# A two-layer encoder trunk on one core: sums of MLP weight blocks made by adding transfers in device memory, with 15 instead of 14 up-projection pairs per layer in seven products

## The reference, cut to what matters

```python
def sq_relu_mlp(y, w_up, w_down):
    u = y @ w_up                              # w_up (1024, 4096), w_down (4096, 1024)
    return jnp.square(jax.nn.relu(u)) @ w_down

for i in range(DEPTH):
    y = rmsnorm(h, norm_gains[i, 0])
    y = mlstm_mixer(y, ...) if i % 2 == 0 else diff_attention(y, ...)
    h = h + y
    h = h + sq_relu_mlp(rmsnorm(h, norm_gains[i, 1]), mlp_w_up[i], mlp_w_down[i])
```

## Time and profile before

| | |
|---|---|
| median of 3 runs | 1207.79 us (1207.68 to 1208.81) |
| the profiled execution's own span | 1205.8 us |
| PE busy | 1195.9 us (99%) |
| DVE busy | 895.2 us (74%) |
| ACT busy | 643.8 us (53%) |
| POOL busy | 62.1 us (5%) |
| DMA | 110.40 MB, 92 GB/s over the span |

### The profile page before, as it was taken

The page is one execution under the profiler, slowest core; times in us unless marked ns, Lnnn a source line. Parts: engine busy times, 40 slices in busy tenths (PEclk is TensorE's granted clock), DMA queues, the critical chain, the costliest instruction groups (busy, mean ns, idle before and its releaser), DMA issues.

```text
span 1205.8 us, 22165 instructions
## 1 busy us (share of the span) xinstructions
PE 1195.9 (99%) x8700; PEld 1133.4 (94%) x8700; DVE 895.2 (74%) x1446; ACT 643.8 (53%) x1117; POOL 62.1 (5%) x105
## 2 busy tenths in 40 slices
PE   9999999999999999999999999999999999999998
PEld 8999999999999999999999999987798998988988
DVE  6788788789479479488568888887984885875863
ACT  6777876744234244234357887777552352443453
POOL 3211120000000000001010000000000000000000
PEclk9999999999999999999999999999999999999999
DMA  7333333232323323323222122212333333242322
GB/s 179 91 100 95 88 91 93 86 95 86 126 71 105 106 71 105 105 73 117 75 81 77 54 70 65 83 44 76 99 105 105 104 107 105 71 141 70 96 79 71
DMA packets 143123, 110.40 MB, mean 92 GB/s; under 512 B 22152, under 2 KB 142016, under 8 KB 143040
## 3 DMA queue, kind: packets, MB, share of 16 engines
q1 hardware_dynamic: 141600, 104.93, 29.2%
q0 software_dynamic: 1312, 4.22, 1.3%
q10 hardware_dynamic: 128, 0.09, 0.0%
HBM read 107.11 MB, written 2.13 MB: 91 GB/s over the span
## 4 chain that ended last, share of the span: by engine, by line
PE 81%; ACT 8%; DVE 6%; issue 3%; DMA 1%; ACTq 0%; DVEq 0%; POOLq 0%
PE ps L2061 32%; PE ps L2115 23%; PE ps L1828 17%; PE ps L2332 2%; ACT dmat L756 1%; PE ps L2188 1%; DVE wl L1176 1%; DVE plo L1317 1%; ACT wh L660 1%; PE ps L2167 1%; PE ps L2166 1%; ACT qhs L660 1%; PE ps L2176 1%; ACT vh L660 1%; ACT phi L660 1%
## 5 line engine op out<-in xcount | busy, mean ns | idle before, releaser
L2061 PE MATMUL ps<-al,hi 128*128 128x264 f32 (+1 forms) x736 | 192.6, 318 | 0.0
L2061 PE MATMUL ps<-ah,hi 128*128 128x264 f32 (+1 forms) x736 | 192.6, 318 | 0.0
L2061 PE MATMUL ps<-ah,lo 128*128 128x264 f32 (+1 forms) x736 | 192.2, 318 | 0.0
L660 ACT ACTIVATE hi<-raw 128x1024 fp32r<-128x1024 f32 (+1 forms) x128 | 119.6, 957 | 133.9 <-PE ps L2061 133.9
L1828 PE MATMUL ps<-yh,wh 128*128 128x264 f32 (+1 forms) x704 | 160.4, 302 | 0.0
L1828 PE MATMUL ps<-yh,wl 128*128 128x264 f32 (+1 forms) x704 | 155.3, 295 | 0.0
L1828 PE MATMUL ps<-yl,wh 128*128 128x264 f32 (+1 forms) x704 | 155.2, 294 | 0.0
L2061 PEld LDWEIGHTS ps<-ah,hi 128*128 128x128 f32 x736 | 121.4, 188 | 10.0
L2061 PEld LDWEIGHTS ps<-al,hi 128*128 128x128 f32 x736 | 121.4, 188 | 9.8
L2061 PEld LDWEIGHTS ps<-ah,lo 128*128 128x128 f32 x736 | 121.2, 188 | 9.8
L2115 PE MATMUL ps<-th,hi 128*128 128x264 f32 (+1 forms) x448 | 126.6, 283 | 0.0
(11 more groups left out here) (295 smaller groups left out, 2729.2 us busy)
## 6 DMA issues: line engine op xcount, KB each, us to landing
raw<-in_mlp_w_up_dram SPq DMA_DIRECT2D x32, 1024.0 KB, 5.4
raw<-in_mlp_w_down_dram SPq DMA_DIRECT2D x32, 1024.0 KB, 5.2
raw<-in_diff_w_in_dram SPq DMA_DIRECT2D x24, 512.0 KB, 3.8
raw<-in_mlstm_w_in_dram SPq DMA_DIRECT2D x16, 512.0 KB, 5.0
raw<-in_mlstm_w_in_dram SPq DMA_DIRECT2D x16, 256.0 KB, 5.5
raw<-in_mlstm_w_out_dram SPq DMA_DIRECT2D x3, 1024.0 KB, 5.2
raw<-in_diff_w_out_dram SPq DMA_DIRECT2D x3, 1024.0 KB, 5.2
nmbc<-gate_rows POOLq DMA_DIRECT2D x8, 264.0 KB, 4.4
```

The source lines that it names most:

```text
L660: return nc.scalar.activation(o, i, ACT.Copy, scale=scale)
L2061: last = mm(ps[:, b + s, 0:cw], x[half][:, 20 * m + kb, :], y[:, kb, c0:c0 + cw], start=(kb == 0 and n == 0), stop=(kb == CB - 1 and n == 2))
```

## The change

1. **Weight sums in device memory.** Two tensors `forms0` and `forms1` in device memory hold S2, S3 (part 0) and S1, S4 (part 1) of all groups of a layer, 8 MiB each. POOL makes them with DMAs. Per group there are four stages: four copies of 512x512 out of `mlp_w_up`; then two transfers that add 512x512 to what is there; then one that adds S1 to S2 in place; then one that adds S2 to S4. Each is 1 MiB. POOL waits for all transfers of a stage before it issues the next. Layer 0's 16 stages are issued two at a time behind POOL's `step0` of heads 0 to 7, layer 1's ahead of each `sql1` and behind the last. The signs of the sums differ from before and are made up for in the inputs (`y_forms`, `forms_hi`, `forms_lo`) and in `total`.
2. **Loads in parts.** SP loads a crossed pair as four parts (S23, A1, S14, A22: 512, 512, 512 and 256 KiB, in pieces of 512 bytes) straight into the place where the low half will stand, each when PE has done with the same part two pairs earlier. S23 and S14 come from `forms`. Plain pairs are two loads of 512 KiB. Pair 1 lands in the memory of `raw`.
3. **Paired products share a bank.** The order is A11, S2, S3, S1, A12, A22, S4; A12 adds onto A11's bank after ACT has copied A11 out, A22 onto S3's and S4 onto S1's. A pair has 6 instead of 7 `total` steps, one of them with the ReLU in it, and four banks of its own parity.
4. **`PLAIN` = 1.** Pair 1 is crossed too: 15 of 16 up pairs per layer.
5. Single-use semaphores at the start are counted on three shared ones. The first weights of layer 1's heads are loaded earlier.

```diff
-PLAIN = 2
+PLAIN = 1
-PRODUCTS = ("A11", "A12", "S2", "S3", "S1", "S4", "A22")
+PRODUCTS = ("A11", "S2", "S3", "S1", "A12", "A22", "S4")
+PARTS = ("S23", "A1", "S14", "A22")
...
+BANK = {"A11": 0, "A12": 0, "S2": 1, "S1": 2, "S4": 2, "S3": 3, "A22": 3}
 def bank_of(i, name):
-    return (7 * (i % 8) + PRODUCTS.index(name)) % 8
+    return 4 * (i % 2) + BANK[name]
...
+            def copied(o, i):
+                pool.dma_start(o, i).then_inc(forms_made, 16)
+            def added(o, i):
+                pool.dma_start(o, i, accum_op=ALU.add, max_dma_last_dim=4096).then_inc(forms_made, 16)
+            def weight_forms(layer, n):
+                g, stage = n // 4, n % 4
+                wait(pool, forms_made, 16 * (8 * (GROUPS * layer + g) + (0, 4, 6, 7)[stage]))
+                up = a["mlp_w_up"][layer]
+                c1, c2 = slice(g * D, g * D + X), slice(g * D + X, g * D + D)
+                s2, s3 = forms[layer][g, 0, 0:X, :], forms[layer][g, 0, X:D, :]
+                s1, s4 = forms[layer][g, 1, 0:X, :], forms[layer][g, 1, X:D, :]
+                if stage == 0:
+                    copied(s1, up[0:X, c2])
+                    copied(s2, up[0:X, c1])
+                    copied(s3, up[0:X, c1])
+                    copied(s4, up[X:D, c1])
+                elif stage == 1:
+                    added(s1, up[X:D, c2])
+                    added(s3, up[0:X, c2])
+                elif stage == 2:
+                    added(s2, s1)
+                else:
+                    added(s4, s2)
             for hd in range(-2, HEADS):
                 step0(hd, hd % 2, hd // 2)
+                if hd >= 0:
+                    weight_forms(0, 2 * hd)
+                    weight_forms(0, 2 * hd + 1)
...
-            with pool.Fori(0, HEADS - 1) as i:
+            for i in range(HEADS - 1):
+                weight_forms(1, 2 * i)
+                weight_forms(1, 2 * i + 1)
                 pool.wait_ge(sq_hi1, i + 1)
                 nc.gpsimd.tensor_tensor(sql1[:, :], abuf[:, NMETA:T], ...)
+            weight_forms(1, 14)
+            weight_forms(1, 15)
...
                     if i == 0:
-                        plain_lo(layer, 1, 0)
-                        plain_lo(layer, 1, 1)
-                        evacuate(0, 0)
+                        part_lo(layer, *e[0])
                         for n in range(4):
                             forms_lo(n)
+                        evacuate(0, 0)
+                        for x in e[1:]:
+                            part_lo(layer, *x)
+                        act_lo(0, 0)
+                        evacuate(0, 1)
+                        continue
```

More of the change, by code:

```diff
@@ L25 @@
+import collections
 from contextlib import ExitStack
@@ L340, in program @@
         gate_rows = nc.dram_tensor("gate_rows", [2 * HEADS, T], F32).ap()
+        forms = [nc.dram_tensor(f"forms{n}", [GROUPS, 2, D, X], F32).ap() for n in range(2)]
         def sem(name):
@@ L1552, in mlp @@
                 for i in range(PAIRS):
+                    this, last = crossed(i), crossed(i - 1)
+                    e = [(i + 1, x) for x in parts(i + 1)] if i + 1 < PAIRS else []
                     if i == 0:
-                        plain_lo(layer, 1, 0)
-                        plain_lo(layer, 1, 1)
-                        evacuate(0, 0)
+                        part_lo(layer, *e[0])
                         for n in range(4):
                             forms_lo(n)
-                    if crossed(i - 1):
-                        total(i - 1, "C21")
-                    elif i > 0 and not is_up(i - 1) and not in_tail(layer, i - 1):
-                        evacuate(i - 1, 1)
@@ new lines, in mlp @@
+                        act_lo(0, 0)
+                        evacuate(0, 1)
+                        continue
+                    if last:
+                        total(i - 1, "C12")
+                        relu(i - 1, 0)
+                    elif not is_up(i - 1) and not in_tail(layer, i - 1):
+                        evacuate(i - 1, 1)
+                    if e:
+                        part_lo(layer, *e[0])
+                    if last:
+                        act_lo(i - 1, 1)
+                    if this:
@@ L1587, in mlp @@
+                    if len(e) > 2:
+                        part_lo(layer, *e[1])
+                    if this:
+                        total(i, "U3")
+                        total(i, "C22")
+                    elif is_up(i):
+                        evacuate(i, 0)
                         act_lo(i, 0)
                         evacuate(i, 1)
-                    elif not is_up(i) and not in_tail(layer, i):
+                    elif not in_tail(layer, i):
+                        if layer == 0 and i == PAIRS - 1:
+                            split(U_IN1, 0)
@@ L1604, in mlp @@
-                    if crossed(i):
-                        total(i, "C12")
-                    if after:
-                        form(i + 2, "S2", 1)
-                    if crossed(i):
-                        relu(i, 0)
-                    if after:
-                        form(i + 2, "S4", 3)
+                        if layer == 0 and i == PAIRS - 1:
+                            split(U_IN1 + 1, 1)
+                    if len(e) == 2:
+                        part_lo(layer, *e[1])
+                    elif e:
+                        part_lo(layer, *e[2])
@@ L1612, in mlp @@
+                    if this:
+                        total(i, "C11")
+                    if len(e) > 2:
+                        part_lo(layer, *e[3])
+                    if this:
+                        total(i, "C21")
+                        relu(i, 1)
                 if layer == 0:
@@ L2115, in product @@
                             last = mm(ps[:, bank, 0:w], x[1 - i % 2][:, row + kb, :], y,
-                                      start=(kb == 0 and n == 0), stop=(kb == 3 and n == 2))
+                                      start=(name in ("A11", "S2", "S3", "S1") and kb == 0 and n == 0),
+                                      stop=(kb == 3 and n == 2), skip_group_check=name in ("A12", "A22", "S4"))
                     last.then_inc(m_done, 1)
```

440 lines of the change are left out of this document (199 added, 241 removed).

## The result

The changed kernel takes **1239.8 us** (median of 4 runs, 1234.4 to 1244.1); the kernel before, on the same chip, 1207.8 (1207.7 to 1208.8). The ratio is 1.026, with a 95% interval of 1.023 to 1.029. The change makes the kernel slower by 32 us, and its runs scatter over 10 us where those of before lie within 1.1.

The account below looks back on a forecast made before the run. PE was taken as the bound, busy for 1195.9 of 1205.8 us. Crossing gain, pair 1's start, transfers and `lamv` summed to 1207.8 - 3.0 + 3.6 + 24 + 4 = 1236 us; range 1203.5 to 1290, the likeliest case's own 1213 to 1255.

Parts of the forecast that it names:

- What bounds the kernel: Whole kernel: PE is the bound; work taken off DVE gains nothing, and any new wait reaching PE is paid in full.
- The transfers on POOL's path: Layer 0's heads: POOL waits for every stage, so masks come late and the heads get 24 us longer.
- An add: POOL's transfers: an adding transfer of 1.05 MB holds the engines for 1.5 copies, 5.1 us, against 3.4 for a copy.
- The fixed parts: POOL's transfers: landing and issue times of a group's four stages, 11.6 us.
- T: Layer 0's heads: time of one group's transfers with SP's weights, 57.7 us, where two heads last 46.2.
- rival 2: All transfers stay under the heads and pair 1's start costs what it gains: 1208.4 us, chance 0.20.
- rival 3: Transfers stay hidden and A1 is not late: 1204.8 us, faster, chance 0.25.
- The first rival: POOL's transfers: an add holds the engines as long as two copies, 6.8 us; 1279 us in all, chance 0.20.
- `lamv` and pair 1's start: Start of MLPs: late `lamv` load costs 4 us in layer 0; A1's late low half 3.6 over both layers.
- The gain of crossing pair 1: Up pair 1 of both layers: crossing saves PE 1.65 us in layer 0 and 1.35 in layer 1, -3.0.
- Layer 1's heads: Layer 1's heads: transfers need 186 us of the 191.4 available before the last `sql1` is late; nothing is lost.
- Edits costed at nothing: Fewer DVE sums, bank sharing, loads in parts, shared semaphores and earlier layer 1 weights: no cost to PE.

Follow-up runs that it names:

- Run 6: Changed kernel with every adding transfer replaced by a same-size copy into its own block, same POOL waits, MLP loading plain blocks: 1212.3 us.
- run 1: Changed kernel without any transfer on POOL; S23 and S14 loaded as plain blocks of the weight matrix: 1210.3 us.
- run 12: Changed kernel without transfers, plain blocks loaded instead of sums, and pair 1 a plain pair again: 1208.8 us.
- run 9: Changed kernel without layer 0's sixteen transfer stages, its MLP loading plain blocks; layer 1's transfers kept: 1212.2 us.
- spread kernels: Changed kernel with one layer 0 stage a head, the other half beside its MLP's down pairs; original start order 1232.7 us, pair 1's A1 first 1231.9.
- run 3: Changed kernel with one layer 0 transfer stage a head, the other half beside the MLP's down pairs, original start order: 1232.7 us.
- run 7: Changed kernel with adds onto blocks of their own and POOL waiting for no transfer; MLP loads plain blocks: 1256.1 us.
- run 5: Changed kernel with layer 0's last two transfer stages issued behind the `lamv` load instead of ahead of it: 1226.1 us.
- run 8: Changed kernel without layer 1's sixteen transfer stages, its MLP loading plain blocks; layer 0's transfers kept: 1237.4 us.
- run 2: Changed kernel without transfers, with pair 1's A1 and S23 halves ahead of the four forms on ACT and DVE: 1209.2 us.

## Why the prediction was right

It said 1236 us, slower, and 1239.8 was measured. The direction and the chain of causes were right; that the size came so near is in good part luck, as the steps show:

- **What bounds the kernel**: right. DVE lost 72 us of work without a gain, and each new wait that reached PE came out in the time. What it left out is that a wait can cost more than its length: 10.8 us at a lower granted clock stand in no term of the sum.
- **The transfers on POOL's path, +24**: the mechanism was right (POOL waits for DMAs on `forms`, masks are late, the share is 0.98; of PE's three waits two, 8.2 us, are behind masks and one, 3.3, behind a late `mbc`), and the term was some 8 us too large: 16.4 in the changed kernel, 13.6 with `lamv` first. Two of its numbers were off in opposite ways. *An add* was taken at 5.1 us, 1.5 copies, because it moves three streams where a copy moves two; measured are 6.0 us, 1.9 copies (a copy 3.2, taken at 3.4). *The fixed parts* were taken at 11.6 us a group in which the engines stand; with the heads' share at 0.98 they stand for about 1 us of 55.7. The engines' work is 4 x 3.2 + 4 x 6.0 = 36.8, SP's weights 15.2, in sum 52.0, and 3.7 us for all the rest. So T was predicted at 57.7 and is 55.7, and (55.7 x 3) - 8.5 - 141.0 = 17.6 is near the 16.4 found. The two errors cancelled, and that is luck: with the measured prices of 3.2 and 6.0 in its own formula T would be 60.7 and the term 33. (For adds at a copy's price the prediction has T = 50.9; its formula gives 50.5.) Run 6, with copies alone, has T at 46.3 or less; with adds at 6.0 rivals 2 and 3, which needed T below 49.8, were out of reach.
- **The first rival (an add as long as two copies), 1279**: its rule fits the runs, its time does not. The Trainium skill ("Collectives: The Full Stack", section on the bandwidth ceiling) says of the adding step of collectives that it runs at half a copy's rate, since its two sources share one read queue. The engine time of 1.9 copies agrees with it; whether a shared queue is the reason, no run here shows. The rival's 43 us in the heads came of a group of 64.9 us, in which the engines stand for most of 11.6; at the measured 3.2 and 6.0 us, and hardly a gap, a group is 55.7.
- **`lamv` and pair 1's start, +4 and +3.6**: the chain was right, with its members and their order. Without late transfers the A1 waits are 1.45 and 2.1 us (1.7 and 1.9 predicted). Behind `lamv` the wait is 8.2, where the two terms gave 5.7: the load was issued at 274.5, not 284, but took 9.0 us to land among the last adds, not 3.4. What the prediction lacked is that PE, once it has stood for those 8.2 us, goes on at a lower granted clock (0.56 in the window from 290 to 300): 2.8 us by windows of 2 us, which is the 2.5 us beyond the wait. The stretch costs 9.6 us against before; the terms for it (1.7 + 4 - 1.65) gave 4.1. At layer 1's start the stretch costs 2.6 where the terms gave 0.55: the wait is the 2.1 us that it is without transfers, but here 1.7 us at a lower clock follow it.
- **The gain of crossing pair 1, -3.0**: as a saving of matmuls it holds, but with waits of 3.5 us it leaves +1.5 (runs 1 and 12) where the prediction's balance was +0.6. Part of the 0.9 us between is how a stall was counted: the waits end at a matmul's recorded end, 0.28 or 0.40 us after its start. In run 1, 1.73 and 2.44 us lie from the last plain start to the first crossed one, where 0.12 and 0.24 lie between starts otherwise, so the two stalls take 3.8 us. The rest has no place.
- **Layer 1's heads, 0**: too low. The prediction allowed 186 us of 191.4. In the trace the three groups take 64.9, 54.3 and 50.1 us, 169.3 where 163.5 were predicted. POOL's last `sql` starts at 838.3, PE waits 2.4 us for it and then runs 1.7 us' worth at a lower clock, and the transfers of layer 1 cost 1.9 us by run 9 (3.6 in the changed kernel's span). The slack was misread too: 5.1 us is that of the `sql` at 709.8. The last one ended at 807.88 + 1.28 = 809.2, and PE took up that product at 811.65, so it had 2.5 (a row of the kernel before):

```profile
811.65 0.40 PE L2207 MATMUL ps<-sqh,head_mean 128*128 128x512 f32 x1
```

- **Edits costed at nothing**: right but for the loads in parts, which by run 12's trace cost PE 1.0 us near the end of the program.

The terms gave +28.6, the span shows +33.1. They came that near because the heads' term, 7.6 too large, stood against four that were too small: layer 0's start by 5.5, the stretch with layer 1's heads by 3.6, layer 1's start by 2.1 and the end by 0.9. The last four have their causes in the trace: a longer `lamv` chain and the lower clock, the `sql` and the clock, the clock, and the late last load. The forecast's sign did not depend on that: it needed only that three groups take longer than 141 us, and they took 167 - 8.5.

My expectation for the spread kernels failed because I took the average share of the MLP's loads for room. The halves of the down matrix are wanted in order and at short notice, and ACT's waits for them grew by 34 us (run 3).

## What to carry to other kernels

Before moving sums from an idle-enough engine to adding transfers, price an add at two copies of engine time (here 6.0 against 3.2 us per MiB), add the loads that share the engines, and compare with the length of the stage; where the sum is over it, every wait behind the issuing queue is paid. Put small loads that someone waits for, as `lamv` here, ahead of a chain of large transfers: moving one stage pair behind it took 9.3 us out of the start of layer 0's MLP. Where a wait reaches PE, look at the granted clock behind it as well. And an engine that is relieved only counts when it was waited for: even with the transfers taken away altogether the change lost 3 us, so there was nothing for them to buy.

## What the runs showed of the hardware that I had not expected

- An adding transfer in device memory holds the DMA engines for 1.9 times as long as a copy of the same bytes; the queue's MB count is the same for both (71.33), and what tells them apart is its share (24.9% and 18.1%) and its packets (22816 and 18720).
- Copies between blocks of device memory went at high rates beside other loads: from 60 to 250 us run 6 has 272 GB/s at a share of 0.89, where the changed kernel, with half of its transfers adding, reached 239 at 0.97.
- The 512 KB loads of another queue land after 5.3 us alone (run 1, median from 60 to 260 us), 12.4 beside copies and adds that wait for each other, 11.3 beside copies alone that do (run 6), and 24.7 beside copies and adds that don't (run 7): the pace of issue, not only the bytes, decides how much others suffer.
- After PE had stood for 8.2 us, the window that followed had a granted clock of 0.56; after 1.45 us at the same place it stayed at 1.00. The length of the wait alone doesn't decide: at layer 1's pair 1 PE stands for 2.1 us in every kernel with the changed kernel's order there. In the changed kernel and in runs 6 and 9 the granted clock was 0.66 to 0.68 in a window of 5 us behind the wait (the row below is the changed kernel's), in runs 1, 3, 5, 7 and 8 it was 1.00. What differs is not shown.

```profile
898.00:903.00 5.00, 4.59 (x26) 4.59 (x27) 4.45 (x7) 4.11 (x8) 0.00 (x0) 0.66 0.50 142
```

- The spread from run to run was at most 2 us in the kernel before and in runs 1, 2 and 6, 10 in the changed kernel and 18 in run 7. A high share of the engines is not enough for it: run 6 has 0.89 in the heads and a spread of 1.3.
